# A combine stage rearranged over four engines: selection pattern built earlier, LayerNorm split between GpSimd, ScalarE and VectorE

## What is computed

```python
y = lax.ragged_dot(act, w_down, group_sizes) + b_down[e_sorted]
y = y * g_sorted[:, None].astype(y.dtype)
out = jnp.zeros_like(xf).at[tok].add(y)
...
h = layer_norm(ALPHA_RES * h + ffn, ln2_g[l], ln2_b[l])
```

## Time and profile before

| | us |
|---|---|
| median of 3 runs (lowest, highest) | 5153.72 (5152.51, 5154.44) |
| the profiled execution, its own time | 5148.1 |
| its span in the trace | 5146.5 |
| combine stage, from its first DMA issue to the end | 4981.0 to 5146.5 |
| placing stage, VectorE from its first to its last operation | 2200.3 to 2226.7 |
| busy over the span: PE, VectorE, ScalarE, GpSimd | 4685.8, 3082.6, 1823.8, 952.7 |

### The profile page before, as it was taken

How to read it: one execution, slowest core, us unless ns; L and a number is a source line. 1 busy time by engine, 2 the same in 40 slices (tenths; PEclk the granted TensorE clock), 3 DMA queues, 4 the chain that set the end, 5 groups by cost and what they waited for, 6 DMA issues and landing times. The chain is left out here.

```text
span 5146.5 us, 68028 instructions
## 1 busy us (share of the span) xinstructions
PE 4685.8 (91%) x23694; PEld 3478.7 (68%) x23695; DVE 3082.6 (60%) x4864; ACT 1823.8 (35%) x2635; POOL 952.7 (19%) x979
## 2 busy tenths in 40 slices
PE   7999678889999986749999999999999999999986
PEld 3444334444444443448999999999999999999961
DVE  2222178788888887156555675556576556666455
ACT  1111123333333332224343443344345434454330
POOL 0000122212111111111111121112122112221127
PEclk9999789999999997869999999999999999999986
DMA  4332210001000000045554555455466455664458
GB/s 186 118 117 109 86 27 18 23 18 20 17 14 14 12 12 9 13 159 197 170 197 155 196 190 179 163 172 202 161 210 225 157 178 189 210 228 157 157 177 322
DMA packets 447421, 663.89 MB, mean 129 GB/s; under 512 B 42624, under 2 KB 306816, under 8 KB 446240
## 3 DMA queue, kind: packets, MB, share of 16 engines
q1 hardware_dynamic: 390768, 515.98, 30.7%
q0 software_dynamic: 26576, 85.56, 4.4%
q10 hardware_dynamic: 29952, 60.83, 3.1%
HBM read 542.92 MB, written 119.38 MB: 129 GB/s over the span
## 5 line engine op out<-in xcount | busy, mean ns | idle before, releaser
L1382 PE MATMUL gu<-x_hi,w_hi 128*128 128x256 f32 (+2 forms) x4096 | 1230.7, 300 | 1.3 <-DVE x_lo L1464 1.3
L1383 PE MATMUL gu<-x_lo,w_hi 128*128 128x256 f32 (+2 forms) x4096 | 1231.3, 301 | 0.0
L1384 PE MATMUL gu<-x_hi,w_lo 128*128 128x256 f32 (+2 forms) x4096 | 1228.5, 300 | 0.0
L1459 DVE TENSOR_TENSOR w_lo<-w_raw,w_hi 128x2048 fp32r<-128x2048 f32 x386 | 874.6, 2287 | 532.6 <-ACT w_hi L1533 532.6
L1533 ACT ACTIVATE w_hi<-w_raw 128x2048 fp32r<-128x2048 f32 x386 | 726.9, 1907 | 282.2 <-PE gu L1384 195.7
L1382 PEld LDWEIGHTS gu<-x_hi,w_hi 128*128 128x128 f32 x4096 | 771.9, 188 | 2.5 <-issue 1.7
L1384 PEld LDWEIGHTS gu<-x_hi,w_lo 128*128 128x128 f32 x4096 | 772.8, 189 | 0.0
L1383 PEld LDWEIGHTS gu<-x_lo,w_hi 128*128 128x128 f32 x4096 | 769.7, 188 | 0.7
L1355 POOL TENSOR_TENSOR a_lo<-up,a_hi 128x384 fp32r<-128x384 f32 x256 | 396.9, 1550 | 1488.1 <-ACT a_hi L1545 1488.1
L1382 PE MATMUL yp<-w_hi,a_hi 128*128 128x512 f32 x1296 | 526.0, 406 | 0.0
L1383 PE MATMUL yp<-w_lo,a_hi 128*128 128x512 f32 x1296 | 514.8, 397 | 0.0
(11 more groups left out here) (256 smaller groups left out, 5429.0 us busy)
## 6 DMA issues: line engine op xcount, KB each, us to landing
w_raw<-w_gate_up SPq DMA_DIRECT2D x258, 1024.0 KB, 8.1
w_raw<-w_down SPq DMA_DIRECT2D x128, 1024.0 KB, 6.4
y_dram<-y_rows ACTq DMA_DIRECT2D x192, 256.0 KB, 3.2
y_dram<-zeros SPq DMA_DIRECT2D x16, 2016.0 KB
h_blk<-h_dram SPq DMA_DIRECT2D x32, 512.0 KB, 6.6
qi_dram<-qi_stage ACTq DMA_DIRECT2D x16, 640.0 KB, 2.9
w_in_sb<-w_in SPq DMA_DIRECT2D x1, 8480.0 KB, 23.7
x_in<-x SPq DMA_DIRECT2D x16, 512.0 KB, 9.3
```

Source lines behind the costliest of these rows:

```text
L1382: nc.tensor.matmul(out, s_hi_, m_hi, start=(n == 0), stop=False)
L1383: nc.tensor.matmul(out, s_hi_, m_lo, start=False, stop=False)
L1384: op = nc.tensor.matmul(out, s_lo_, m_hi, start=False, stop=(n == len(pairs) - 1))
L1459: nc.vector.tensor_tensor(w_lo[:, c % 2, cols], raw[:, c % 3, cols], w_hi[:, c % 2, cols].bitcast(F32), ALU.subtract).then_inc(s_lo, 1)
```

## The change

Four things are done, in `combine_stage` unless said otherwise.

1. `mine` moves from the stage's own buffers to `S["mine"]`, and is built by GpSimd at the end of its stream in `place_stage`. With it go one memset, two `affine_select` and two drains, and the semaphore `s_made` on which `g_sum` waited.
2. GpSimd now issues gathers 0 to 3 together, then the memset of `minus_half`, then a `drain`. Its wait for the constants goes. For each tile it issues gather t + 4 first, then waits for the variance, does the power, a `drain`, mean times inverse deviation, a `drain`, and the sign change. It adds no bias any more.
3. ScalarE applies mean and deviation: an `Identity` with scale and bias by row over 128 x 1024.
4. VectorE does the sums and statistics of tile t, and behind them gain and bias of tile t - 1, with a drain between the two.

```diff
--- before.py
+++ after.py
@@ -63,6 +63,7 @@
 META = MAX_VISITS + 1
 TAIL = 8 * P
 CHUNK = 4096
+CUT = P // TOP_E
 
 
 def wait(eng, sem, value):
@@ -1138,6 +1139,13 @@
                                allow_small_or_imprecise_dtypes=True).then_inc(s_made, 1)
                 nc.gpsimd.iota(visit_no[:], pattern=[[1, META]], base=0, channel_multiplier=0,
                                allow_small_or_imprecise_dtypes=True).then_inc(s_made, 1)
+                nc.gpsimd.memset(S["mine"][:], 1.0)
+                pool.drain()
+                nc.gpsimd.affine_select(out=S["mine"][:], in_=S["mine"][:], compare_op=ALU.is_ge, fill=0.0, base=0,
+                                        pattern=[[-TOP_E, CUT]], channel_multiplier=1)
+                pool.drain()
+                nc.gpsimd.affine_select(out=S["mine"][:], in_=S["mine"][:], compare_op=ALU.is_gt, fill=0.0, base=TOP_E,
+                                        pattern=[[TOP_E, CUT]], channel_multiplier=-1)
 
             @block.tensor
             def _(pe):
@@ -1603,26 +1611,22 @@
             return ctx.enter_context(nc.semaphore(name))
 
         AHEAD, SUMS, OUTS = 4, 3, 3
-        CUT = P // TOP_E
-
         gain = sb("gain_2", [P, D])
         bias = sb("bias_2", [P, D])
         b_down = sb("b_down_sb", [EXPERTS, D])
         rows = sb("rows", [P, AHEAD, TOP_E, D])
         h1 = sb("h1_blk", [P, AHEAD, D])
-        mine = sb("mine", [P, CUT])
         g_sum = sb("g_sum", [P, TILES, TOP_E, CUT])
         by_pick = sb("by_pick", [P, TILES, TOP_E, EXPERTS])
         by_expert = sb("by_expert", [P, TILES, EXPERTS])
         by_expertT = sb("by_expertT", [EXPERTS, TILES, P])
         total = sb("total", [P, OUTS, D])
-        small = sb("small2", [P, OUTS, 16])
+        small = sb("small2", [P, OUTS, 17])
         minus_half = sb("minus_half2", [P, 1])
         acc = ctx.enter_context(nc.psum_tensor("c_acc", [P, SUMS, D], F32))
         trp = ctx.enter_context(nc.psum_tensor("c_tr", [P, 2, 4, P], F32))
 
         s_const = sem("c_const")
-        s_made = sem("c_made")
         s_h1 = [sem(f"c_h1{n}") for n in range(AHEAD)]
         s_rows = [sem(f"c_rows{n}") for n in range(AHEAD)]
         s_by = sem("c_by")
@@ -1674,26 +1678,21 @@
 
                 pool.wait_ge(S["relayed"], 64)
                 gather(0)
-                nc.gpsimd.memset(minus_half[:], -0.5)
-                nc.gpsimd.memset(mine[:], 1.0)
-                pool.drain()
-                nc.gpsimd.affine_select(out=mine[:], in_=mine[:], compare_op=ALU.is_ge, fill=0.0, base=0,
-                                        pattern=[[-TOP_E, CUT]], channel_multiplier=1)
-                pool.drain()
-                nc.gpsimd.affine_select(out=mine[:], in_=mine[:], compare_op=ALU.is_gt, fill=0.0, base=TOP_E,
-                                        pattern=[[TOP_E, CUT]], channel_multiplier=-1).then_inc(s_made, 1)
                 for t in range(1, AHEAD):
                     gather(t)
-                pool.wait_ge(s_const, 48)
+                nc.gpsimd.memset(minus_half[:], -0.5)
+                pool.drain()
                 for t in range(TILES):
                     slot = t % OUTS
-                    pool.wait_ge(s_var, t + 1)
-                    nc.gpsimd.tensor_tensor(small[:, slot, 15:16], small[:, slot, 14:15], minus_half[:], ALU.pow
-                                            ).then_inc(s_rstd, 1)
+                    mean, var_eps, rstd, shift = (small[:, slot, j:j + 1] for j in (12, 14, 15, 16))
                     if t + AHEAD < TILES:
                         gather(t + AHEAD)
-                    pool.wait_ge(s_norm, t + 1)
-                    nc.gpsimd.tensor_tensor(total[:, slot], total[:, slot], bias[:], ALU.add).then_inc(s_out, 1)
+                    pool.wait_ge(s_var, t + 1)
+                    nc.gpsimd.tensor_tensor(rstd, var_eps, minus_half[:], ALU.pow)
+                    pool.drain()
+                    nc.gpsimd.tensor_tensor(shift, mean, rstd, ALU.mult)
+                    pool.drain()
+                    nc.gpsimd.tensor_scalar(shift, shift, -1.0, 1.0, ALU.mult, ALU.mult).then_inc(s_rstd, 1)
 
             @block.tensor
             def _(pe):
@@ -1733,18 +1732,16 @@
                 nc.vector.tensor_reduce(by_expert[:], by_pick[:].rearrange("p t k e -> p t e k"), AX, ALU.add
                                         ).then_inc(s_by, 1)
                 dve.wait_ge(S["relayed"], 64)
-                dve.wait_ge(s_made, 1)
                 shape = [P, TILES * TOP_E, CUT]
                 nc.vector.tensor_tensor(g_sum[:].rearrange("p t k c -> p (t k) c"),
-                                        mine[:].unsqueeze(1).broadcast_to(shape),
+                                        S["mine"][:].unsqueeze(1).broadcast_to(shape),
                                         S["gate_by_pick"][:].unsqueeze(2).broadcast_to(shape), ALU.mult
                                         ).then_inc(s_gd, 1)
                 dve.wait_ge(s_const, 48)
 
-                for t in range(TILES):
+                def sums(t):
                     slot, at = t % OUTS, t % AHEAD
-                    stats, mean_var = small[:, slot, 0:12], small[:, slot, 12:14]
-                    var_eps, rstd = small[:, slot, 14:15], small[:, slot, 15:16]
+                    stats, mean_var, var_eps = small[:, slot, 0:12], small[:, slot, 12:14], small[:, slot, 14:15]
                     if t >= OUTS:
                         dve.wait_ge(s_st[slot], 16 * (t // OUTS))
                     dve.wait_ge(s_h1[at], 16 * (t // AHEAD + 1))
@@ -1758,11 +1755,19 @@
                     nc.vector.bn_aggr(mean_var, stats)
                     dve.drain()
                     nc.vector.tensor_scalar(var_eps, mean_var[:, 1:2], EPS, None, ALU.add).then_inc(s_var, 1)
-                    dve.wait_ge(s_rstd, t + 1)
-                    nc.vector.tensor_scalar(total[:, slot], total[:, slot], mean_var[:, 0:1], rstd,
-                                            ALU.subtract, ALU.mult)
-                    dve.drain()
-                    nc.vector.tensor_tensor(total[:, slot], total[:, slot], gain[:], ALU.mult).then_inc(s_norm, 1)
+
+                def affine(t):
+                    slot = t % OUTS
+                    dve.wait_ge(s_norm, t + 1)
+                    nc.vector.tensor_tensor(total[:, slot], total[:, slot], gain[:], ALU.mult)
+                    dve.drain()
+                    nc.vector.tensor_tensor(total[:, slot], total[:, slot], bias[:], ALU.add).then_inc(s_out, 1)
+
+                for t in range(TILES):
+                    sums(t)
+                    if t:
+                        affine(t - 1)
+                affine(TILES - 1)
 
             @block.scalar
             def _(act):
@@ -1770,6 +1775,11 @@
                     act.wait_ge(s_bt, g + 1)
                     nc.scalar.activation(by_expertT[:, 4 * g:4 * g + 4], trp[0:EXPERTS, g % 2], ACT.Copy
                                          ).then_inc(s_bts, 1)
+                for t in range(TILES):
+                    slot = t % OUTS
+                    act.wait_ge(s_rstd, t + 1)
+                    nc.scalar.activation(total[:, slot], total[:, slot], ACT.Identity, bias=small[:, slot, 16:17],
+                                         scale=small[:, slot, 15:16]).then_inc(s_norm, 1)
 
 
 def build(nc, A, upto=9):
@@ -1807,6 +1817,7 @@
         S["pos"] = sb("pos", [P, TILES, TOP_E], I32)
         S["pos_by_pick"] = sb("pos_by_pick", [P, SEQ * TOP_E // P], I32)
         S["gate_by_pick"] = sb("gate_by_pick", [P, SEQ * TOP_E // P])
+        S["mine"] = sb("mine", [P, CUT])
         S["relayed"] = ctx.enter_context(nc.semaphore("relayed"))
         place_stage(nc, A, S, D_)
         experts_stage(nc, A, S, D_)
```

## The result

The change makes the kernel slower: median 5220.02 us of 4 runs (5218.63 to 5222.47) against 5153.11 of 4 runs before; ratio 1.0133 with a 95% interval of 1.012 to 1.0145, or 67 us. The forecast was slower by 41 us, 5195, with a range to 5215. The direction and the mechanism held; the size did not.

What follows compares the result with a forecast made beforehand. GpSimd sets the pace at 8.42 us a tile, DMA within 1 us. Gather 15 at 5015.2 + 11 x 12.0, drain to 5159.0, 28.8 behind it: 5187.8, 41 above the span; with the difference to the median 5195, range 5165 to 5215.

Steps and rivals of the forecast that it cites:

- The drain: GpSimd, combine stage: a drain waits until its own indirect DMAs have landed; read from one drain of 16.7 us.
- rival (a): GpSimd's drain does not wait for gathers; DMA bounds at 7.4 to 8.1 us a tile, about 5132 us; chance 0.12.
- The hole: Start of combine stage: GpSimd held between memset of `mine` (4988.09) and first `affine_select` (4999.79), by the drain between them.
- The start: Combine stage: first drain waits for gather 3, gather 4 starts about 5015.2 against 5018.1; 12 us of hole bring 3.
- The period: GpSimd, each tile: landing 11.0, drain 0.2, product and sign 0.55, next issue 0.2; about 12.0 us against 8.42.
- the upper bound: Period at most 14.2 us: landing 12.1, 0.95 behind it, up to two further issues lengthened by 0.6 each.
- The 0.6 us of the shared port: A gather's second issue takes 1.56 us, not 0.95, beside VectorE's two-operand multiplication; up to 1.2 us a period, upper bound only.
- an estimate of 8.5 us for a landing: Landing from the skill's 2.0 us plus bytes over 436 GB/s; period 9.5, total +12 us; set aside for measured landings.
- the prediction's own formula: Whole kernel: the end is 5043.8 plus 12 times the period, level with before at a period of 8.6 us.
- ScalarE and VectorE: Combine stage: ScalarE's `Identity` 1.24 us, VectorE's sums 3.10 and gain and bias 2.5 a tile; hidden while GpSimd waits.
- (b): GpSimd's drain waits, but for less; period 8.4 to 9.4, -2 to +10 us, about 5158 us; chance 0.04.
- (c): DMA already at its limit, pace stays 8.4, only start and longer tail show; about 5154 us; chance 0.02.

Runs made afterwards that it cites:

- the kernel with semaphores: Changed kernel with no drain left in the combine stage: minus_half set before gather 0, power, product and sign each ordered by a semaphore; 5121.4 us, ratio 0.9949.
- the kernel without transfers: Changed kernel, drains kept, without the stores of tiles 0 to 12 and the h1 loads of tiles 4 to 15; 5178.6 us, ratio 1.0054.

## Why the prediction was right and wrong

**The drain.** "A drain on GpSimd waits until its own indirect DMAs have landed" was read from one drain of 16.7 us. It holds in every kernel that has a drain behind a gather, and those without one do not show the wait; rival (a), with its 12 in 100, is out. The hole's cause is settled too: without that drain it is gone. The direction was no luck: it came from this reading, and the added drain alone costs what the reading says.

**The start.** Gather 4 was put at 5015.2; it started at 5020.15, or 5016.0 once the 4.1 us of the later stage are taken off. The pattern at no cost in the placing stage held: its two selects take 0.21 us each there, under VectorE.

**The period: the step that failed.** It was the term "Output and h1 share the window now as they will then", by which the landing of before, 11.0 us, was carried over. It measured 13.3. The store of a tile hangs on the deviation, which now comes right before the next gather, and through ScalarE and VectorE 3.4 us after its first issue. The "about 4 us" between deviation and store stood in the same text, in the part on VectorE, and the 3.3 us before a gather's data in the part on the period; laid side by side they say that the transfers meet the gather at its height. The prediction did not lay them side by side. The mean of all eleven periods is 14.3 ((5177.63 - 5020.15) / 11), just past the upper bound of 14.2, and the range had been cut at 13.7: the upper bound came from landings of before, all of which had the transfers ahead of the gather, so it bounded the wrong case. The 11.0 was also taken as free of any influence of a neighbour gather, and was not quite: with transfers ahead and no gather overlapping the next (the kernel before with one drain added) it is 10.3. What makes up these 0.7 us is not shown.

**The sum, term by term,** to the span, 5219.5 against 5187.8: landing 2.3 us more for each of gathers 5 to 15, 25; the wait behind it 1.3 us instead of 0.95 in twelve periods (an issue behind the sign starts after 0.49 us, not 0.2), 4; gather 4, which met no store, 1.5 less; the start 0.8 more; the tail 27.9 instead of 28.8, 0.9 less; and the later stage, 4.1. Together 31.5 of 31.7. In the medians 25 us remain: the changed kernel's profiled execution, 5221.0, was 1.0 above its median, and that of before 5.6 below the median that the prediction used.

**The 0.6 us of the shared port.** The second issue takes 1.52 us beside VectorE's multiplication (5061.74 beside 5061.21), as in the earlier trace rows; the bias added no second one to the changed kernel. In the kernel with semaphores the issue takes 1.85 us. At the end of the stage the power takes 1.46 us (5198.53) beside VectorE's gain (5198.37), against 0.58 elsewhere. By the Trainium skill (SBUF — State Buffer, SBUF: two separate sides) VectorE and GpSimd shut each other out of one port pair; these rows agree. What the longer issue costs a landing is not settled. With the store 1.2 us behind the first issue, a second issue of 0.95 us went with a landing of 12.0 and one of 1.8 us with 11.7, so nothing shows there; but gather 4 of the changed kernel, with four short issues and no store beside it, landed in 9.5 us, and the kernel without transfers, with the longer issue, took 10.0. The fixed cost and rate in the Trainium skill (DMA: Bandwidth & Descriptors, Anatomy of one DMA) made an estimate of 8.5 us for a landing; the kernel without other transfers took 10.0, so it falls short even there. (The total that goes with that estimate is 11 us by the prediction's own formula, not 12.)

**ScalarE and VectorE** were priced right: 1.24 us, and 3.1 + 2.5 us a tile. Rivals (b) and (c) are out.

## What to carry to other kernels

Before a drain is put into a loop, ask what else this engine has in flight: on GpSimd it waits for the engine's own gathers, so that no gather overlapped the next here, in spite of four buffers; order two instructions with a semaphore that the first one raises, which cost less than 0.1 us here. And when a new wait empties a shared resource, the neighbours' latencies measured in the full pipeline can't be carried over: work out anew, from the event that releases each transfer, when it will fall against the one that is waited for.

## What the runs showed of the hardware

- GpSimd's drain covers indirect DMAs that GpSimd issued (11.6 to 12.2 us in the median, 0.76 us in tile 12 of the changed kernel, the first with no gather in flight). For SP's plain DMAs the runs show no such wait (L1345 in the earlier trace rows, with the weights streaming), though none was made for it.
- A wait on the engine's own semaphore lets the next small instruction start 0.1 us after the one before (5053.95 + 0.58 to 5054.62).
- A 2.1 MB gather alone lands 10.0 us behind its first issue, 5.4 of it issuing; 0.5 MB of store and 0.5 MB of load in its window add 1.5 to 1.9 us each.
- With GpSimd ahead, the 16 DMA engines kept 419 GB/s over 40 us, at a share of 1.03.
